# Moving the row-index step and the row-code products of the extra expert units

## The reference, cut to what matters

```python
grp_prob = softmax(t @ w_rg + b_rg);  grp_p, grp_idx = top_k(grp_prob, 1)
exp_logits = (t @ w_re + b_re).reshape(-1, 4, 4)
top_logits, top_local = top_k(in_group, 2)          # two experts of the chosen group
weights = grp_p * softmax(top_logits)
act = silu(einsum('td,edf->tef', t, w_gate[e])) * einsum('td,edf->tef', t, w_up[e])
out = out + einsum('tef,efd->td', act * combine[:, e, None], w_down[e])
```

## Time and profile before

| | us |
|---|---|
| median of three runs | 893.41 |
| lowest, highest | 888.84, 895.46 |
| the profiled execution, whole time | 889.86 |
| its span | 888.1 |
| PE busy | 765.7 (86%) |
| DVE busy | 548.5 (62%) |
| ACT busy | 397.1 (45%) |

### The profile page before, as it was taken

One profiled execution on the slowest core, in us unless ns is written; L12 is line 12 of the kernel. 1 busy time (PEld: TensorE's weight loads), 2 busy tenths in 40 slices (PEclk: granted clock), 3 DMA queues, 4 the chain that ended last, 5 costly groups with the idle time before them and its releaser, 6 DMA issues.

```text
span 888.1 us, 10265 instructions
## 1 busy us (share of the span) xinstructions
PE 765.7 (86%) x3870; PEld 608.5 (69%) x3872; DVE 548.5 (62%) x834; ACT 397.1 (45%) x616; POOL 70.2 (8%) x130
## 2 busy tenths in 40 slices
PE   6999997986998989989989899986789889999930
PEld 5787676775767767767758688765567777778720
DVE  5689675444435535435346618586758878889717
ACT  7247733333212212212234314335358778888722
POOL 7000000000000000000000000010011222122100
PEclk9999998997999999999989999888789999999975
DMA  6444121010110110201111291446679999999515
GB/s 197 143 96 94 50 94 48 1 48 0 48 48 1 48 48 9 87 1 48 48 47 48 96 373 54 142 142 206 207 257 329 339 335 338 340 341 332 200 62 221
DMA packets 66499, 123.53 MB, mean 139 GB/s; under 512 B 19801, under 2 KB 41362, under 8 KB 66450
## 3 DMA queue, kind: packets, MB, share of 16 engines
q1 hardware_dynamic: 59744, 114.44, 38.0%
q0 software_dynamic: 6624, 8.41, 2.7%
q10 hardware_dynamic: 82, 0.03, 0.0%
HBM read 122.32 MB, written 16.25 MB: 156 GB/s over the span
## 4 chain that ended last, share of the span: by engine, by line
PE 70%; DVE 10%; DMA 9%; issue 5%; ACT 3%; POOL 1%; DVEq 0%; SPq 0%; ACTq 0%; POOLq 0%
PE bank L1362 15%; PE bank L1364 15%; PE bank L1363 14%; DMA unit_tokens<-ffn_rows,row_index 8%; PE bank L1553 3%; PE bank L1561 2%; PE bank L1559 2%; PE bank L1712 2%; PE bank L1586 1%; PE bank L1587 1%; DVE dn L1067 1%; DVE dn L1089 1%; PE bank L1456 1%; DVE down_lo L1151 1%; PE bank L1671 1%
## 5 line engine op out<-in xcount | busy, mean ns | idle before, releaser
L1362 PE MATMUL bank<-h_hi,w_hi 128*128 128x512 f32 x304 | 130.5, 429 | 1.5 <-DVE h_lo L891 1.5
L1364 PE MATMUL bank<-h_hi,w_lo 128*128 128x512 f32 x304 | 120.3, 396 | 0.0
L1363 PE MATMUL bank<-h_lo,w_hi 128*128 128x512 f32 x304 | 119.8, 394 | 0.0
L1151 DVE TENSOR_TENSOR gate_up_lo<-ew_raw,gate_up_hi 128x1024 fp32r<-128x1024 f32 x92 | 108.0, 1216 | 0.5 <-ACT gate_up_hi L797 0.3
L797 ACT ACTIVATE gate_up_hi<-ew_raw 128x1024 fp32r<-128x1024 f32 x92 | 91.8, 1052 | 0.0
L874 DVE TENSOR_TENSOR w_lo<-w_raw,w_hi 128x2048 fp32r<-128x2048 f32 x26 | 59.5, 2287 | 30.8 <-ACT w_hi L618 30.8
L1362 PE MATMUL bank<-gate_up_hi,unit_in_hi 128*128 128x512 f32 x184 | 76.2, 414 | 0.0
L583 POOL DMA_INDIRECT unit_tokens<-ffn_rows,row_index x23 | 29.3, 1275 | 569.3 <-DVE row_index L1269 553.9
L1364 PE MATMUL bank<-gate_up_hi,unit_in_lo 128*128 128x512 f32 x184 | 72.4, 394 | 0.0
L1363 PE MATMUL bank<-gate_up_lo,unit_in_hi 128*128 128x512 f32 x184 | 72.2, 392 | 0.0
L1362 PEld LDWEIGHTS bank<-h_hi,w_hi 128*128 128x128 f32 x304 | 58.3, 192 | 14.7 <-issue 3.3
(11 more groups left out here) (353 smaller groups left out, 1506.8 us busy)
## 6 DMA issues: line engine op xcount, KB each, us to landing
ew_raw<-in_w_gate SPq DMA_DIRECT2D x46, 512.0 KB
ew_raw<-in_w_up SPq DMA_DIRECT2D x46, 512.0 KB
ew_raw<-in_w_down SPq DMA_DIRECT2D x46, 512.0 KB
w_raw<-in_w_in SPq DMA_DIRECT2D x17, 1024.0 KB, 5.2
w_raw<-in_w_out SPq DMA_DIRECT2D x4, 1024.0 KB, 5.1
expert_rows<-expert_rows_hbm SPq DMA_DIRECT2D x8, 512.0 KB, 6.7
x_T<-in_x SPq DMA_DIRECT2D x4, 512.0 KB, 5.4
w_raw<-in_w_in SPq DMA_DIRECT2D x8, 256.0 KB, 4.3
```

The costliest lines, as they stand in the source:

```text
L1151: dve.tensor_tensor(dst, eraw[slot][:, :], hi.bitcast(F32), ALU.subtract).then_inc(elo_done, 1)
L1362: pe.matmul(out_ap, lhs_hi, rhs_hi, start=first, stop=False)
L1363: pe.matmul(out_ap, lhs_hi, rhs_lo, start=False, stop=False)
L1364: return pe.matmul(out_ap, lhs_lo, rhs_hi, start=False, stop=last)
```

## The change

Two blocks move; nothing is added or removed. On DVE, `row_ids(3+u)` and `one_hots(4+u)` go from ahead of the down low part to the end of the unit, behind the up low part. On PE, `row_codes(3+u)` goes from behind `gate_up(u)` to ahead of it, behind `unit_in(u+1)` and ahead of the waits of `gate_up(u)`.

```diff
                 if u == 0:
                     extra_units()
-                if 1 <= u <= 4:
-                    row_ids(3 + u)
-                    if u < 4:
-                        one_hots(4 + u)
                 if u:
                     split_expert_lo(KIND_D, u - 1)
                     dve.wait_ge(hid_hi, u)
@@
                 if 0 < u < UNITS - 1:
                     split_expert_lo(KIND_U, u + 1)
+                if 1 <= u <= 4:
+                    row_ids(3 + u)
+                    if u < 4:
+                        one_hots(4 + u)
@@ tensor
                 if u + 1 < UNITS:
                     unit_in(u + 1)
+                if 1 <= u <= 4:
+                    row_codes(3 + u)
                 pe.wait_ge(elo_done, place(KIND_U, u)[2])
                 pe.wait_ge(xs_lo_done, u + 1)
                 if u >= 2:
@@
                 gate_up(u, range(KT // 2, KT))
-                if 1 <= u <= 4:
-                    row_codes(3 + u)
                 if u:
                     down(u - 1)
```

## The result

The changed kernel takes 880.20 us in the median of four runs (877.22 to 881.02), against 891.97 us before (888.84 to 895.46) in the same comparison. The ratio is 0.9861 with a 95% interval of 0.9815 to 0.9907, so 11.8 us saved. Timed twice more, each time beside the kernel before, it gave 877.21 against 893.47 us (0.9815, 0.9784 to 0.9846) and 878.24 against 894.19 us (0.9814, 0.9783 to 0.9845). The forecast was 869.5 us with a range of 862 to 878. The sign was right and the gain too large: the 22 us of the forecast were 11.8 in the first comparison and 16.3 and 16.0 in the two later ones.

What follows compares the result with a forecast made beforehand. The prediction took a ring of waits between DVE and PE to bound units 1 to 4; 22.5 us saved there less 0.5 lost behind gave 22, so 867.9 to 871.4 us, forecast at 869.5, range 862 to 878.

Steps and rivals of the forecast that it cites:

- The ring of waits: Units 1 to 4: DVE waits 15.5 us for row codes, PE 16.6 us for DVE; the change removes both.
- the forecast's floor: Units 1 to 4 at DVE's floor of 10.45 us each: `gate_up(5)` starts at 638.0 instead of 661.9, 23.9 us saved.
- The cost at unit 1: PE waits 1.2 us for one-hots of batch 4, then does codes in 1.0; `gate_up(1)` starts 2.4 us later.
- One-hots in time for units 2 to 4: One-hots come within 0.3 us of when PE wants them in units 2 to 4; taken as no cost.
- DVE's floor of 10.45 us: DVE's work per unit, 8.92 us plus 1.53 for ids and one-hots, sets the period if data come in time.
- PE's floor: PE's work per unit without waits: 9.34 us plus about 1.0 for codes, 10.35 us, a little under DVE's.
- P = 10.8 between 10.45 and 11.4: Period of units 1 to 4, between DVE's floor and the two-unit gather loop; `gate_up(5)` at 639.4, 22.5 us saved.
- Nothing much lost from unit 5 on (0.5 us): Behind units 1 to 4 the loop keeps its old pace, losing 0.5 us because the DMA queues won't have rested.
- The bytes: The stretch's 13.3 MB take 39.7 us at 336 GB/s, just under the 40.3 us available, so DMA runs almost full.
- given back to the transfers: Rival, chance 0.12: late gathers hold P at 11.4 and cost 0.3 us on each of 17 later units; 875 us.
- the rival's P of 19.2: Rival "slower", chance 0.03: waits ahead of `gate_up` keep the clock at 1.2 GHz through units 1 to 4; 901 us.
- P's upper bound: Two-unit gather loop, 13.6 us plus a gather of 9.14, is 22.7 us, or 11.4 a unit; 20.1 us saved.

Runs made afterwards that it cites:

- the early pair: `early_before` and `early_after`: the kernel before and the changed kernel, each with gathers issued one unit earlier, ahead of the scatter; 876.99 and 854.64 us.
- `half_weights`: Changed kernel with expert weights from unit 2 on loaded only by their first half, so output is not the layer's; one run, 852.33 us.
- `dve_only`: Kernel before with only the DVE block moved (ids and one-hots to the end of DVE's unit); 877.78 us, ratio 0.9839.
- `after_third`: Changed kernel as it is, timed again beside the PE half alone; 878.24 us, ratio 0.9814 to the kernel before.
- `early_pe`: Kernel before with only the PE block moved, plus gathers issued one unit earlier, ahead of the scatter; 854.87 us, ratio 0.9549.
- `pe_only_again`: Kernel before with only the PE block moved (row codes ahead of `gate_up`), timed again beside the whole change; 873.26 us, ratio 0.9775.

## Why the prediction was right in its mechanism and wrong in its size

- *The ring of waits, and that it opens:* right. DVE's wait for the codes is gone, and of PE's waits ahead of down products one is left, 4.7 us at the loop's end (841.97 us), outside the stretch that the change touches. Without late gathers units 1 to 5 gain 24.3 us where the forecast's floor gave 23.9.
- *The cost at unit 1:* right. PE waits 1.12 us for the one-hots (1.2 forecast), and `gate_up(1)` starts 1.0 us behind that.
- *One-hots in time for units 2 to 4:* right, no wait of PE for them.
- *DVE's floor of 10.45 us sets the period:* wrong, and harmless by luck. DVE's own period is 10.20 us (gate low part at 609.14 to the next at 619.34, no idle time between), since the step from the input low part to the down low part is 1.20 us there and not 1.44. PE's floor, forecast at 10.35, sets the pace: 10.37 from `gate_up` to `gate_up`, 10.39 from silu 1 to silu 2. The two floors lie so close that the sum hardly moves.
- *P = 10.8 between 10.45 and 11.4:* this is the step that failed. From silu 1 to silu 5 the four steps sum to 49.2 us, 12.3 each, where the forecast with its shorter last units has (4 x 10.8 - 1.5) / 4 = 10.4. Three terms of the gather's loop were too small. First, L, the time from the start of a gather's issue to its landing: I took 8.4 and "the first gathers are early", but the first gather queued behind a scatter, unit 4's, took 9.24 us, 1.02 of them its held-up issue. Second, the 3.5 us from the last down product to the gather's start were 4.45 for unit 4 (608.24 to 612.69), as the scatter's issue too was held up by 0.97. Third, the forecast knew that a gather wait of about 3 us had let the clock fall once, and put that only into a rival, and there only for later units. Here it fell in unit 3 already, for 2.8 us. With these in the forecast's own sum, the loop of two units is 4.45 + 9.24 + 10.1 = 23.8 us and P is 11.9; four of them less 1.5, with 2.8 for the fall, make 48.9, against the 49.2 measured. The second gather that PE waits for, unit 6's, was a little quicker (9.04), so the last 0.3 us are not accounted for one by one.
- *Nothing much lost from unit 5 on (0.5 us):* too small in two of the three profiles, which have 0.3 us gained, 3.0 lost and 4.5 lost; the early pair has 2.3 lost. Here too the clock fell behind late gathers: behind waits of 2.71 and 2.82 us in the first profile (steps of 13.9 and 14.0 us, granted clock 0.76 from 669 to 676 and 0.79 from 714 to 722).
- *The bytes:* wrong. 336 GB/s was taken as the DMA engines' limit and the period was checked against it. With early gathers they moved 363 to 367, so the rate of before was held down by the gather waits. The load still is one of the two things that make a gather late, as `half_weights` shows.
- *The rivals:* "given back to the transfers", at a chance of 0.12, had the right mechanism. Its saving of 15 us lies between the 11.8 and the 16.3 measured, but by parts that were not so: 20.1 in units 1 to 4 and 5.1 lost behind, where 13 to 15 and up to 4.5 were measured. That the clock would stay down through units 1 to 4 did not happen (the rival's P of 19.2 adds up to 19.05, which changes nothing): in units 1 to 5 it fell behind one wait of 3.13 us and not behind those of 2.82 and 1.12 us. The length of the wait alone does not decide: in `dve_only` it fell behind a wait of 2.28 us (granted clock 0.55 from 620.2 to 624) and in `after_third` behind one of 1.83 (0.52 from 781.5 to 785). The Trainium skill's page on the clock gate ("TensorE: Matmul & The Clock Gate", section "HAM oscillation — how this bites in real kernels") is borne out in part: a wait in front of a bunch of matmuls did let the clock fall, but not every time.
- *The range:* its upper end, 878, came from P's upper bound with no fall of the clock in it and a loop that was too short. The later medians, 877.2 and 878.2, lie at that end and not in the middle, so they bear out the sign and not the sum.

## What to carry to other kernels

When a wait is taken away, go round the next loop with the new, shorter period: here a loop over two units (output copy, scatter issue, gather, transposes) had room at 16.7 us a unit and none at 10.4. A load that needs nothing of a result should not be queued behind that result's store; moving the gathers one place ahead in POOL's order was worth 14 us by itself and let the whole 22 of this change through, 854.6 us in all, with `early_pe` the fastest of the kernels here that compute the whole layer. And a throughput seen in a stretch where something waits is no upper bound for that stretch.

## What the runs showed of the hardware

An indirect DMA issued from POOL took 1.01 us to issue where DVE was idle, read PSUM, or started an instruction at the same moment (`pe_only_again`, 611.57 and 633.61), and 1.4 to 2.04 us where DVE was already making a low part from two SBUF operands; what it took more was about the rest of that instruction. Unit 4's gather, from the start of a 2.03 us issue to its landing, took 9.24 to 9.50 us beside the full weight loads, 7.10 when nearly all its rows were left out, and 6.30 when the weight loads had half their bytes. The DMA engines moved 363 to 367 GB/s over 138 us in a loop whose rate had stood at about 336 GB/s as long as PE waited for gathers. The granted clock fell from its upper to its lower level behind waits of PE of 1.83, 2.28 and 3.13 us; of two waits of 2.82 us in one profile, it fell behind one (714.32) and stayed up behind the other (648.05). One fall, with 12 of a unit's 24 products at the lower level, cost 2.4 to 2.8 us.
